# Wide bf16 products of the identity in the waits of TensorE through the heads loop of a three-layer block kernel

## Chip, cores and metric

One core of one Trainium2 chip runs the whole program. The metric is the device time of one execution in microseconds (us), the median of several; smaller is better. The profile shows one execution on the same core. Engine names: PE is TensorE's matmul, PEld its weight load, DVE VectorE, ACT ScalarE, POOL GpSimd, SP SyncE.

## What is computed

The reference runs one sequence of 256 tokens of width 1024 through three layers: a gated delta rule mixer with 16 value heads and 8 key heads of width 128, a forgetting attention with 16 heads of width 64, and a block with window attention, pooling and a layer of 16,384 small experts. The change touches the first alone, and of it the part per head:

```
g = cumsum(g);  decay = exp(where(lower, g_t - g_s, -inf))
L = where(strict, (k*beta) @ k.T * decay, 0)
T = inverse(I + L)                  # unit lower triangular
u, w = T @ (v*beta), T @ (k*beta*exp(g))
v_new = u - w @ state;  o = (q*exp(g)) @ state + (q @ k.T * decay) @ v_new
state = state * exp(g_last) + k_dec.T @ v_new
```

The kernel takes chunks of 128 tokens, two per sequence, where the reference has 64; the result is the same.

## The kernel before, in words

The program is written by hand for each engine, with semaphores between them: within an engine the order of the code is the order of the work. Every projection is made of fp32r products of high and low parts. The input projection of the delta rule runs until about 195 us, then comes the **heads loop**, then the output projection.

The heads loop has 8 rounds (`rounds(inner)`, L2544). A round takes one key head and its two value heads g = 0, 1. In `inner(i, f, n)` (L2496) three rounds are in flight: `i` is the one whose triangular matrices are inverted, `f` the one before it, which is finished, and `n` the one after, which is set up. So round 0 has no `f`, and round 7 has no `n`; the finish of round 7 stands after the loop, between the output products.

The inverse of the four 128x128 matrices (two heads, two chunks) is built up in six levels j = 0 to 5, from blocks of 2 to one of 128. A level has two halves. `level_p(r, j)` (L2413) waits for the semaphores `h_xx` (the matrix so far, `XC` and its transpose `XC_T`) and writes into the PSUM bank PA; DVE's `mask_level` (L1648) masks it into SBUF and fires `h_pm`; `level_d(r, j)` (L2438) multiplies again into the bank PB; DVE's `close_level` (L1660) subtracts and fires `h_xx`, twice a level (three times at level 4, once at level 5, 12 in a round). For j < 4 each half is 16 products of 32x32 blocks (PE L2424 and L2451, two records each), at j = 4 it is 8 and 12 small ones (L2429; L2456, L2458), at j = 5 four of 64x64 (L2434, L2462). DVE's parts of them: L1653 is the mask of levels 0 to 3, L1656 of level 4, L1658 of level 5; L1664 closes levels 0 to 3, L1669 and L1671 level 4, L1674 level 5.

Between these halves PE does the rest of the three rounds in a fixed order:

- `finish(f, 0)` to `finish(f, 5)` (L2466): 128x128 fp32 products, steps 0, 1, 2, 3 at L2474, L2478, L2481, L2484, step 4 with three products for each head (L2489 to L2491), step 5 at L2494. The copies between them are ACT's (L965 after step 0, L968 after step 1).
- `setup_keys(n)` (L2375), `setup_rows(n)` (L2364; two bf16 products of 512 columns at L2372, a selector column against BG3), `setup_values(n)` (L2388; four transposes at L2393), `setup_low(n)` (L2399; 16 small products at L2402, after DVE's `lowers`, L1638).
- `modulator(i)` (L2406; two fp32 products of one column at L2410, of rows that POOL has summed) and, while `i.at + 2 < 8`, `norm_sums` (L2352; one fp32 product of 512 columns at L2356, which the trace shows as two).

BG3 is a bf16 tile of 128 rows by 512 columns that holds the gate rows in high, middle and low parts (48 of the 128 rows; the rest is zero); it is written before the loop and only read in it. `ident16` is the 128x128 identity in bf16. `mm` is `pe.matmul(out, stationary, moving)`. A PSUM bank is 512 fp32 columns; PA is ps[2], PB is ps[3].

At round 7 ACT has work of another kind: `late_silu` (L896), for which it loads another table of functions (L898) and then the old one again (L752). DVE and ACT also split the operand of the output projection into parts in that round (L1405, L766).

`keep_clock` (L2286) makes small fp32 products of the identity at three places outside the loop; the loop has none.

Of the kernel before, what the change touches and what calls it, by code (L numbers as in the profile page):

```python
# [51 lines left out]
def program(nc, x, c, norm_w, ada_w, ada_b, a_w_in, a_conv_w, a_A_log, a_dt_bias, a_norm_w, a_w_out,  # L52
# [4 lines left out]
    with ctx:  # L57
# [3 lines left out]
        def sem(name):  # L61
            return ctx.enter_context(nc.semaphore(name))
# [11 lines left out]
        def at(off, n, tensor=AR):  # L74
            return tensor[:, off:off + n]
# [14 lines left out]
        def small(n, p=P):  # L90
            pos[0] += n
            assert pos[0] <= 2624, pos[0]
            return SMALL[0:p, pos[0] - n:pos[0]]
# [3 lines left out]
        ident16 = small(64).bitcast(B16)  # L97
# [78 lines left out]
        h_p, h_pm, h_d, h_xx = sem("h_p"), sem("h_pm"), sem("h_d"), sem("h_xx")  # L176
# [156 lines left out]
        BG3 = at(T0 + 10496, 256).bitcast(B16)  # L333
# [32 lines left out]
        PA, PB, PBC = ps[2], ps[3], ps[3][:, 256:320]  # L366
# [1861 lines left out]
        def _(pe):  # L2228
            mm = pe.matmul
# [134 lines left out]
            def setup_rows(r):  # L2364
                pe.wait_ge(g_kks, r.count(1, 1))
                pe.wait_ge(g_kqs, r.count(1, 1))
                pe.wait_ge(g_k0s, r.count(1, 1))
                if r.at:
                    pe.wait_ge(h_bv, r.count(4))
                for g in range(2):  # L2370
                    h = r.heads[g]
                    mm(ROWS[g][:, :], SELB[:, h:h + 1].broadcast_to([P, P]), BG3, start=True, stop=True).then_inc(h_row, 1)  # L2372

            def setup_keys(r):
                pe.wait_ge(g_norm, r.count(2, 2))  # L2375
                pe.wait_ge(ada_free, r.count(1, 9))
                if r.at == 0:
                    pe.wait_ge(g_ln, 2)
                for cc in range(2):
                    kc = r.k[:, cc * 128:cc * 128 + 128]  # L2380
                    ins = mm(KKP[:, cc * 128:cc * 128 + 128], kc, kc, start=True, stop=True)
                ins.then_inc(g_kk, 1)
                for cc in range(2):
                    chunk = slice(cc * 128, cc * 128 + 128)
                    mm(KQP[:, cc * 128:cc * 128 + 128], r.k[:, chunk], r.q[:, chunk], start=True, stop=True)
                pe.transpose(K0P, r.k[:, 0:128], ident).then_inc(g_k0, 1)

            def setup_values(r):  # L2388
                for g in range(2):
                    pe.wait_ge(h_eg, r.nth(g))  # L2390
                    pe.wait_ge(h_xm, r.nth(g))
                    for cc in range(2):
                        ins = pe.transpose(ROWS[g][:, 256 + cc * 128:384 + cc * 128], r.v[g][:, cc * 128:cc * 128 + 128], ident)  # L2393
                    ins.then_inc(h_vT, 1)

            def diagonal_blocks():
                return [(m, q, m // 2, 128 * (m % 2) + q) for m in range(4) for q in (0, 32, 64, 96)]

            def setup_low(r):  # L2399
                pe.wait_ge(h_lt, r.nth(1))  # L2400
                for m, q, g, at_ in diagonal_blocks():
                    ins = mm(LOWC[q:q + 32, 32 * m:32 * m + 32], LT[r.side][g][q:q + 32, at_:at_ + 32], ident[q:q + 32, q:q + 32],  # L2402
                             start=True, stop=True)
                ins.then_inc(h_xT, 1)

            def modulator(r):  # L2406
                pe.wait_ge(mod_sum, r.count(15, 24 + 15))
                pe.wait_ge(ada_free, r.count(1, 10))
                for cc in range(2):
                    ins = mm(MODP[:, cc:cc + 1], RAW[MOD_SLOT[r.side]][:, 0, cc * 128:cc * 128 + 128], ones[:, 0:1], start=True, stop=True)  # L2410
                ins.then_inc(raw_free, 1)

            def level_p(r, j):  # L2413
                lt = LT[r.side]
                if j == 0:
                    pe.wait_ge(h_xt, r.count(3, 2))
                elif j < 5:
                    pe.wait_ge(h_xx, r.count(12, 2 * j - 1))
                else:
                    pe.wait_ge(h_xx, r.count(12, 9))  # L2420
                    pe.wait_ge(h_spread, r.count(6, 2))
                if j < 4:
                    for m, q, g, at_ in diagonal_blocks():
                        ins = mm(PA[q:q + 32, 32 * m:32 * m + 32], lt[g][q:q + 32, at_:at_ + 32], XC[q:q + 32, m, :],  # L2424
                                 start=True, stop=True)
                elif j == 4:
                    for m, q, g, at_ in diagonal_blocks():
                        if q % 64 == 0:
                            ins = mm(PA[q + 32:q + 64, 32 * m:32 * m + 32], lt[g][q:q + 32, at_ + 32:at_ + 64], XC[q:q + 32, m, :],  # L2429
                                     start=True, stop=True)  # L2430
                else:
                    for m in range(4):
                        at_ = 128 * (m % 2)
                        ins = mm(PA[64:128, 64 * m:64 * m + 64], lt[m // 2][0:64, at_ + 64:at_ + 128], XPAIR[0:64, m, :],  # L2434
                                 start=True, stop=True)
                ins.then_inc(h_p, 1)

            def level_d(r, j):  # L2438
                pe.wait_ge(h_pm, r.count(6, j + 1))
                if j == 0:  # L2440
                    pe.wait_ge(h_xt, r.count(3, 3))
                    if r.at:
                        pe.wait_ge(h_xx, r.count(12))
                elif j < 5:
                    pe.wait_ge(h_xx, r.count(12, 2 * j))
                else:
                    pe.wait_ge(h_xx, r.count(12, 11))
                    pe.wait_ge(h_spread, r.count(6, 4))
                if j < 4:
                    for m, q, g, at_ in diagonal_blocks():  # L2450
                        ins = mm(PBC[q:q + 32, 16 * m:16 * m + 16], XC_T[q:q + 32, m, :], PC[q:q + 32, 16 * m:16 * m + 16],  # L2451
                                 start=True, stop=True)
                elif j == 4:
                    for m in range(4):
                        pm = PC[:, 32 * m:32 * m + 32]
                        mm(PB[32:64, 32 * m:32 * m + 32], XC_T[32:64, m, :], pm[32:64, :], start=True, stop=True)  # L2456
                        for q in (0, 64):
                            ins = mm(PB[q:q + 32, 128 + 32 * m:160 + 32 * m], pm[q + 32:q + 64, :], XC_T[q + 32:q + 64, m, :],  # L2458
                                     start=True, stop=True)
                else:  # L2460
                    for m in range(4):
                        ins = mm(PB[0:64, 64 * m:64 * m + 64], XPAIR[64:128, m, :], INVT[r.side][64:128, m, 64:128],  # L2462
                                 start=True, stop=True)
                ins.then_inc(h_d, 1)
# [30 lines left out]

            def inner(i, f, n):  # L2496
                level_p(i, 0)
                level_d(i, 0)
                if f:
                    finish(f, 0)  # L2500
                level_p(i, 1)
                if f:
                    finish(f, 1)
                if n:
                    setup_keys(n)
                level_d(i, 1)
                if f:
                    finish(f, 2)
                level_p(i, 2)
                if n:  # L2510
                    setup_rows(n)
                level_d(i, 2)
                if f:
                    finish(f, 3)
                level_p(i, 3)
                if f:
                    finish(f, 4)
                level_d(i, 3)
                if n:
                    setup_values(n)  # L2520
                level_p(i, 4)
                level_d(i, 4)
                if f:
                    finish(f, 5)
                if n:
                    setup_low(n)
                level_p(i, 5)
                modulator(i)
                if i.at + 2 < GQ:
                    norm_sums(Round(i.at + 2))  # L2530
                level_d(i, 5)
# [203 lines left out]
            for half in range(2):  # L2735
                for b in range(2):
                    for kk in range(4 * half, 4 * half + 4):
                        for n, (w, xx) in enumerate(((WHI, XHI), (WHI, XLO), (WLO, XHI))):
                            ins = mm(bank(T_AUP, 3)[:, b * S:b * S + S], w[:, slot, kk, b * P:b * P + P], xx[:, (kk + 4) % KC, :],
                                     start=(kk == 0 and b == 0 and n == 0), stop=(kk == KC - 1 and n == 2), skip_group_check=True)  # L2740
# [4 lines left out]
            for half in range(2):  # L2745
                pe.wait_ge(x_split, 17 + half)
                for t in range(TT):
                    for kk in range(4 * half, 4 * half + 4):
                        for n, (xx, w) in enumerate(((XHI, WHI), (XLO, WHI), (XHI, WLO))):
                            ins = mm(bank(T_WO, 0)[:, t * TW:t * TW + TW], xx[:, (kk + 4) % KC, t * P:t * P + P], w[:, slot, kk, :],  # L2750
                                     start=(kk == 0 and t == 0 and n == 0), stop=(kk == KC - 1 and n == 2), skip_group_check=True)
# [158 lines left out]
```

## Time and profile before

| | us |
|---|---|
| median of 3 runs | 1623.2 |
| lowest and highest | 1621.7, 1625.29 |
| time of the profiled execution | 1621.4 |
| its span, first to last instruction | 1619.6 |
| mean granted TensorE clock in it | 0.987 of full |
| PE busy | 1554.8 |
| DVE busy | 1109.9 |
| ACT busy | 932.7 |

The share of busy PE is high over the span, but a busy PE isn't one at its peak: the matmuls are pipelined and their ends are modelled, so the time from one start to the next tells more than a duration. In the chain of waits a piece runs until the next one of the chain begins, so its pieces add up. The granted clock is given as a share of full speed: 1.00 is 2.4 GHz, 0.50 is 1.2 GHz.

### The profile page before, as it was taken

To read this page: it belongs to the slowest core of one execution; us is meant where nothing else is said; L and a number is where in the kernel's file an instruction comes from. 1 tells how busy PE (TensorE), PEld (TensorE's weight loads), DVE (VectorE), ACT (ScalarE), POOL (GpSimd) and SP (SyncE) were. 2 spreads that over 40 slices of the span, in tenths; PEclk is the share of its full clock that TensorE was granted. 3 is DMA by queue.
4 is the path that set the end of the run, shared out by engine and by line. 5 is a ranking of instruction groups with operands and counts; after the bars stand their busy time and mean duration, and the time that the engine had idled before them with its cause. 6 is when DMAs were issued, how large, how long until landed. Compare 5 with 4: busy or idle time off the path is not lost.

```text
span 1619.6 us, 37025 instructions
## 1 busy us (share of the span) xinstructions
PE 1554.8 (96%) x13269; PEld 1429.3 (88%) x13269; DVE 1109.9 (69%) x2304; ACT 932.7 (58%) x1763; POOL 493.4 (30%) x405
## 2 busy tenths in 40 slices
PE   7899999899999999999999999999999999999998
PEld 6899877798998899888999999999999888888886
DVE  3787768656556653776478888798888555555554
ACT  1766567744555555545354444799898544555554
POOL 4000278661000040000067777766565100000000
PEclk9999979899999999999999999999999999999999
DMA  9668412454443344247455555544444666666663
GB/s 295 219 184 278 150 55 82 133 163 130 151 131 118 111 156 131 79 157 156 104 150 167 168 168 172 162 143 135 140 131 143 182 194 194 193 192 190 194 193 127
DMA packets 211832, 255.89 MB, mean 158 GB/s; under 512 B 15912, under 2 KB 193804, under 8 KB 211724
## 3 DMA queue, kind: packets, MB, share of 16 engines
q1 hardware_dynamic: 211723, 254.39, 53.2%
q8 instruction: 76, 1.25, 0.3%
q14 instruction: 33, 0.26, 0.1%
HBM read 253.29 MB, written 1.05 MB: 157 GB/s over the span
## 4 chain that ended last, share of the span: by engine, by line
PE 72%; DVE 11%; issue 5%; DMA 4%; ACT 4%; SPq 2%; DVEq 0%; ACTq 0%
PE ps L2253 22%; PE ps L2861 22%; PE ps L2843 10%; PE ps L2831 3%; DMA raw<-in_u_experts 3%; PE ps L2273 2%; PE ps L2551 2%; DVE raw L2014 2%; SPq L580 2%; PE ps L2628 1%; DVE w_lo L1396 1%; PE ps L2451 1%; DMA arena<-in_ada_w 1%; DVE arena L2067 1%; PE ps L2648 1%
## 5 line engine op out<-in xcount | busy, mean ns | idle before, releaser
L742 POOL TENSOR_TENSOR w_lo<-raw,w_hi 128x1024 fp32r<-128x1024 f32 x128 | 307.6, 2406 | 337.7 <-ACT w_hi L1265 337.6
L2253 PE MATMUL ps<-x_hi,w_hi 128*128 128x256 f32 x1088 | 315.3, 290 | 8.3 <-DVE w_lo L1396 3.0
L2253 PE MATMUL ps<-x_hi,w_lo 128*128 128x256 f32 x1088 | 308.2, 283 | 0.0
L2253 PE MATMUL ps<-x_lo,w_hi 128*128 128x256 f32 x1088 | 308.2, 283 | 0.0
L2212 DVE TENSOR_TENSOR w_lo<-raw,w_hi 128x1024 fp32r<-128x1024 f32 x124 | 152.0, 1226 | 143.2 <-ACT w_hi L1374 143.2
L1374 ACT ACTIVATE w_hi<-raw 128x1024 fp32r<-128x1024 f32 x124 | 131.6, 1061 | 168.0 <-PE ps L2861 168.0
L2253 PEld LDWEIGHTS ps<-x_hi,w_hi 128*128 128x128 f32 x1088 | 209.1, 192 | 15.3 <-issue 6.0
L2253 PEld LDWEIGHTS ps<-x_lo,w_hi 128*128 128x128 f32 x1088 | 209.2, 192 | 1.3 <-issue 1.2
L2253 PEld LDWEIGHTS ps<-x_hi,w_lo 128*128 128x128 f32 x1088 | 209.0, 192 | 0.0
L1265 ACT ACTIVATE w_hi<-raw 128x1024 fp32r<-128x1024 f32 x128 | 134.9, 1054 | 113.4 <-DVE raw L2014 113.2
L2806 PE MATMUL ps<-x_hi,w_hi 128*128 128x256 f32 x576 | 166.3, 289 | 10.6 <-ACT arena L1287 9.7
L2014 DVE STREAM_TRANSPOSE raw<-raw 128x1024 f32<-128x1024 f32 x128 | 158.3, 1237 | 17.1 <-DMA raw<-in_u_experts 15.8
L2806 PE MATMUL ps<-x_lo,w_hi 128*128 128x256 f32 x576 | 162.8, 283 | 0.0
L2806 PE MATMUL ps<-x_hi,w_lo 128*128 128x256 f32 x576 | 162.7, 282 | 0.0
L2861 PE MATMUL ps<-w_hi,x_hi 128*128 128x512 f32 x512 | 157.6, 389 | 1.1 <-DVE x_lo L2202 1.1
L2861 PE MATMUL ps<-w_lo,x_hi 128*128 128x512 f32 x512 | 157.7, 389 | 0.0
L2861 PE MATMUL ps<-w_hi,x_lo 128*128 128x512 f32 x512 | 157.6, 389 | 0.0
L1396 DVE TENSOR_TENSOR w_lo<-arena,w_hi 128x2048 fp32r<-128x2048 f32 (+1 forms) x43 | 97.1, 2258 | 70.0 <-ACT w_hi L759 70.0
L1396 DVE TENSOR_TENSOR w_lo<-raw,w_hi 128x2048 fp32r<-128x2048 f32 (+1 forms) x43 | 97.2, 2261 | 69.3 <-ACT w_hi L759 69.3
L2843 PE MATMUL ps<-x_lo,w_hi 128*128 128x256 f32 x448 | 131.9, 294 | 0.0
L2843 PE MATMUL ps<-x_hi,w_hi 128*128 128x256 f32 x448 | 126.7, 283 | 0.0
L2843 PE MATMUL ps<-x_hi,w_lo 128*128 128x256 f32 x448 | 126.5, 282 | 0.0
(446 smaller groups left out, 3563.7 us busy)
## 6 DMA issues: line engine op xcount, KB each, us to landing
raw<-in_u_experts SPq DMA_DIRECT2D x512, 128.0 KB, 2.7
raw<-in_v_experts SPq DMA_DIRECT2D x128, 512.0 KB, 4.3
arena<-in_ada_w SPq DMA_DIRECT2D x18, 1024.0 KB, 7.8
raw<-in_a_w_in SPq DMA_DIRECT2D x12, 1024.0 KB, 5.7
arena<-in_a_w_in SPq DMA_DIRECT2D x12, 1024.0 KB, 5.7
raw<-in_b_w_in SPq DMA_DIRECT2D x8, 1024.0 KB, 5.7
arena<-in_b_w_in SPq DMA_DIRECT2D x8, 1024.0 KB, 5.6
raw<-in_w_in SPq DMA_DIRECT2D x8, 1024.0 KB, 5.6
```

The lines of the kernel that those rows point to most:

```text
L580: sp.dma_start(URAW[u][32 * q:32 * q + 32, :].rearrange("p (a c) -> p a c", a=4), src).then_inc(u_in[u], 16)
L742: pool.tensor_tensor(UTL[e], UT[e % 2], UTH[e].bitcast(F32), ALU.subtract).then_inc(utl_ready, 1)
L1265: act.activation(UTH[e % 4], UT[e % 2], ACT.Copy).then_inc(uth_ready, 1)
L1374: act.activation(VH[u], VRAW[u], ACT.Copy).then_inc(high_ready, 1)
L1396: v.tensor_tensor(WLO[:, slot, 0:k, :], RAW[raw_slot(base, u)][:, 0:k, :], WHI[:, slot, 0:k, :].bitcast(F32), ALU.subtract).then_inc(lo_re ...
L2014: v.transpose(UT[s_].rearrange("p (k a j) -> p a k j", k=KC, a=4), URAW[s_].rearrange("p (a k i) -> p a k i", a=4, k=KC)).then_inc(ut_read ...
L2212: v.tensor_tensor(VL[u], VRAW[u], VH[u].bitcast(F32), ALU.subtract).then_inc(low_ready, 1)
L2253: ins = mm(o[:, b * S:b * S + S], w[:, slot, kk, b * P:b * P + P], xx[:, (kk + turn) % KC, :], start=(kk == 0 and n == 0), stop=(kk == k - ...
L2806: ins = mm(ps[e % 2][:, 0:S], w[e % 4][:, kk * P:kk * P + P], xx[:, kk, :], start=(kk == 0 and n == 0), stop=(kk == KC - 1 and n == 2))
L2831: ins = mm(GB.rearrange("p (e t) -> p t e", t=4)[:, q, :], OHJ[:, c % 2, q, :], OHI[:, c % 2, q, :], start=True, stop=True, skip_group_che ...
L2843: ins = mm(ps[e % 2][:, 0:S], w[e % 4][:, kk * P:kk * P + P], xx[:, kk, :], start=m == 0, stop=m == 23)
L2861: ins = mm(ps[4 + 2 * t + h][:, :], g[:, u, t * P:t * P + P], w[u][:, 512 * h:512 * h + 512], start=False, stop=False, skip_group_check=True)
```

## The change

A helper `keep_wide(bank_, n)` issues n products of `ident16` with BG3 over the whole of a PSUM bank, whose result nobody reads. `level_p` calls it on PA before its waits, `level_d` on PB before its wait for `h_pm`; the number is an argument, `spare`, given in `inner` by the place in the round and by whether there is an `f` or an `n`. In `level_d` at level 0 the wait for the last `h_xx` of the round before moves ahead of it, since the products overwrite PB.

```diff
--- before.py
+++ after.py
@@ -2410,8 +2410,13 @@
                     ins = mm(MODP[:, cc:cc + 1], RAW[MOD_SLOT[r.side]][:, 0, cc * 128:cc * 128 + 128], ones[:, 0:1], start=True, stop=True)
                 ins.then_inc(raw_free, 1)
 
-            def level_p(r, j):
+            def keep_wide(bank_, n):
+                for _ in range(n):
+                    mm(bank_[:, :], ident16, BG3, start=True, stop=True)
+
+            def level_p(r, j, spare=0):
                 lt = LT[r.side]
+                keep_wide(PA, spare)
                 if j == 0:
                     pe.wait_ge(h_xt, r.count(3, 2))
                 elif j < 5:
@@ -2435,12 +2440,13 @@
                                  start=True, stop=True)
                 ins.then_inc(h_p, 1)
 
-            def level_d(r, j):
+            def level_d(r, j, spare=0):
+                if j == 0 and r.at:
+                    pe.wait_ge(h_xx, r.count(12))
+                keep_wide(PB, spare)
                 pe.wait_ge(h_pm, r.count(6, j + 1))
                 if j == 0:
                     pe.wait_ge(h_xt, r.count(3, 3))
-                    if r.at:
-                        pe.wait_ge(h_xx, r.count(12))
                 elif j < 5:
                     pe.wait_ge(h_xx, r.count(12, 2 * j))
                 else:
@@ -2495,36 +2501,36 @@
 
             def inner(i, f, n):
                 level_p(i, 0)
-                level_d(i, 0)
+                level_d(i, 0, 2)
                 if f:
                     finish(f, 0)
-                level_p(i, 1)
+                level_p(i, 1, 0 if f else 2)
                 if f:
                     finish(f, 1)
                 if n:
                     setup_keys(n)
-                level_d(i, 1)
+                level_d(i, 1, 0 if n else 1)
                 if f:
                     finish(f, 2)
-                level_p(i, 2)
+                level_p(i, 2, 0 if f else 2)
                 if n:
                     setup_rows(n)
-                level_d(i, 2)
+                level_d(i, 2, 0 if n else 2)
                 if f:
                     finish(f, 3)
-                level_p(i, 3)
+                level_p(i, 3, 0 if f else 2)
                 if f:
                     finish(f, 4)
-                level_d(i, 3)
+                level_d(i, 3, 0 if f else 2)
                 if n:
                     setup_values(n)
-                level_p(i, 4)
-                level_d(i, 4)
+                level_p(i, 4, 0 if n else 2)
+                level_d(i, 4, 1)
                 if f:
                     finish(f, 5)
                 if n:
                     setup_low(n)
-                level_p(i, 5)
+                level_p(i, 5, 0 if f else 2)
                 modulator(i)
                 if i.at + 2 < GQ:
                     norm_sums(Round(i.at + 2))
```

## Rows read from the trace of the kernel before

**Rows 1.** The page's first line, the profiled execution:

```profile
span 1619.6 us, 37025 instructions
```

**Rows 2.** Chosen stretches: length, busy us (instructions) by engine, granted clock, DMA share, GB/s:

```profile
203.10:220.20 17.10, 15.23 (x276) 11.97 (x277) 8.26 (x25) 7.73 (x25) 14.35 (x22) 0.50 0.21 64
...
290.20:293.60 3.40, 3.40 (x86) 2.42 (x86) 3.17 (x10) 2.88 (x8) 3.40 (x7) 1.00 0.11 24
305.50:308.90 3.40, 2.68 (x85) 2.28 (x84) 3.17 (x10) 3.27 (x10) 3.40 (x7) 1.00 0.80 257
308.90:322.60 13.70, 11.95 (x252) 10.14 (x252) 5.78 (x17) 7.74 (x15) 6.46 (x9) 0.50 0.77 245
```

**Rows 3.** Timeline of PE, round 0: start us, us, line, operation, shapes, idle before:

```profile
197.20 0.44 PE L2451 MATMUL ps<-arena 32*32 32x16 f32 x32 [0.43 <-DVE arena L1653]
197.99 0.45 PE L2424 MATMUL ps<-arena 32*32 32x32 f32 x32 [0.35 <-DVE arena L1664]
...
201.02 0.61 PE L2372 MATMUL ps<-arena,small 128*128 128x512 bf16 x2 [0.20 <-DVE arena L1627]
201.56 0.44 PE L2451 MATMUL ps<-arena 32*32 32x16 f32 x32
```

**Rows 4.** Chain that ended last, rounds 0 to 2, 5, 6: start us, us, what:

```profile
203.47 0.63 PE ps L2451 x32
204.10 1.04 PE ps L2393 x4
205.14 0.59 PE ps L2429 x16
...
207.51 0.65 PE ps L2402 x32
...
214.02 0.63 PE ps L2451 x32
...
222.04 0.64 PE ps L2484 x4
...
223.48 0.22 PE ps L2490 x2
...
224.60 0.37 PE ps L2451 x32
224.97 0.59 PE ps L2393 x4
225.56 0.39 PE ps L2429 x16
...
231.34 0.33 DVE arena L1674
...
231.86 0.44 PE ps L2451 x32
...
279.05 0.44 PE ps L2451 x32
...
294.34 0.44 PE ps L2451 x32
```

**Rows 5.** Timeline of PE, end of round 1 (columns as in rows 3):

```profile
227.76 0.45 PE L2402 MATMUL ps<-small,arena 32*32 32x32 f32 x32
...
230.25 0.68 PE L2462 MATMUL ps<-arena 64*64 64x64 f32 x8
```

**Rows 6.** Chain that ended last, round 7 (columns as in rows 4):

```profile
310.77 1.28 ACT L752
...
312.39 1.22 PE ps L2478 x4
...
319.91 0.43 PE ps L2490 x2
...
322.94 0.46 PE ps L2429 x16
```

**Rows 7.** Waits of PE, 196 to 330: line, releaser, total us, times, longest:

```profile
PE ps L2456 <- DVE arena L1656: 3.2, 8, 0.4
```

## The prediction

> **What bounds the kernel now.** I read three things in this order: the page's head, then the granted clock of chosen stretches, then the chain of work that ended last beside the timeline of PE. The profiled execution spans 1619.6 us [rows 1]; the program's own time for it is 1621.4, so 1.8 us lie around the span, and it stands 1.8 us under the median of the runs, 1623.2. I take all savings against that execution and subtract their sum from the median. About 0.2%, 3.2 us, is what a measurement of this kernel can tell from no change.
>
> The clock: over 203.1 to 220.2 and over 308.9 to 322.6 TensorE was granted 0.50 of full speed, its 1.2 GHz level; elsewhere in the loop, as at 290.2 and 305.5, 1.00, which is 2.4 GHz [rows 2]. The first lies over the end of round 0 and most of round 1, the second over round 7. What the engine did before the second fall can be set beside a twin: 305.5 to 308.9 belongs to the same part of round 6 as 290.2 to 293.6 of round 5, 15.3 us earlier. There the clock held. Both have a PE busy most of the time by instructions [rows 2], but only the earlier one holds the two 512-column products of `norm_sums`, which rounds 6 and 7 leave out; the later has only 32- and 64-row blocks and the one-column products of `modulator`. So what I read is that small blocks don't keep the clock and wide products do. Round 0 has no `finish` work of an earlier round, so it too is nearly all small blocks.
>
> The chain: in the loop it alternates between PE products and short DVE masks in round 0, and runs almost wholly over PE from d0 to p4 in rounds 1 to 6 (I call level_p and level_d at step j of a round p_j and d_j). Start to start from the d0 of round 1 to that of round 2 is 231.86 - 214.02 = 17.84 us, the first part at the low clock; from round 5 to round 6 it is 294.34 - 279.05 = 15.29 [rows 4].
>
> **The change.** Nothing is removed. It adds 39 products of the bf16 identity with BG3, 512 columns each: 13 in round 0, 3 in each of rounds 1 to 6 (a pair in d0, one in d4), 8 in round 7 (d0 2, d1 1, d2 2, p4 2, d4 1). It moves one wait: in d0 of rounds 1 to 7 the wait for `h_xx` now stands before the pair, since the pair overwrites PB. No DMA, no SP or POOL instruction moves.
>
> *Price of a pair.* The nearest row is `setup_rows`, two bf16 128x128 by 512-column products: 201.02 to the next start at 201.56, 0.54 us at the full clock [rows 3]. A single one is then 0.27. They have different stationary operands; the new ones share theirs, so it could be a little less. By the Trainium skill (TensorE: Matmul & The Clock Gate, Back-to-back issue gap) a sustained stream of 512-column products has about 131 ns each, a pair 0.26; the rows have twice that, and I keep the rows.
>
> *Round 0 before the fall.* The pairs at d0, p1, p2, p3 and d3 stand in waits for DVE. d0 starts at 197.20 and p1 at 197.99, 0.79 apart [rows 3], of which a 32-block level issues for 0.37 (at 224.60) [rows 4]; 0.42 is left for 0.54. So +0.12 each at p1 and p2, and about as little at d0 (0.03); p3's is swallowed, since DVE computes `decays` there, and so is d3's. Sum +0.27.
>
> *Round 0 from 203.1, if the clock holds.* Cold against warm durations of the same work: d3 0.63 to 0.37, `setup_values` 1.04 to 0.59, p4 0.59 to 0.39: -0.91 [rows 4]. Then DVE, unchanged. From `setup_low` at 207.51 to the d0 of round 1 at 214.02 it took 6.51 [rows 4]. Warm: `setup_low` to d5 is 230.25 - 227.76 = 2.49 [rows 5]; add the pair at p5, 0.54; d5 itself, 0.68; DVE's L1674, at least 0.33 [rows 4] and with its handovers 0.5; the pair of d0, 0.54: 4.75. That is -1.76. With the +0.27 the stretch gives **-2.4**.
>
> *Round 1, d0 to d0.* 17.84 becomes 15.29: **-2.55**.
>
> *The pair in d0, rounds 2 to 6.* This is the cost. L1674 on DVE ends at 231.34 + 0.33 = 231.67 and fires `h_xx`; the mask follows, and d0 starts at 231.86 [rows 4]. So the moved wait leaves a gap of 0.19 us and not more, and 0.54 must fit in it: +0.35 per round. Behind it on PE stands d0, and everybody waits for d0, since from here the chain is PE's. Five rounds, **+1.75**. Bounds: nothing (it fits) to 0.54 each, 2.7 in all; I take 0.35 because both ends of the gap are rows. The d0 of round 7 is hidden: the next finish step there starts at 312.39 because ACT loads tables and does the late silu until 312.05 [rows 6]. The single in d4 stands in the eight waits for DVE's L1656, 3.2 us in total, 0.4 each after the modelled end of the products [rows 7]; it costs 0.
>
> *Round 7, if the clock holds.* Up to 312.39 ACT sets the pace and nothing is gained. From there to p4 at 322.94 the PE issues finish steps 1, 2 and 3, each four pieces, at 1.22 us cold against 0.64 warm: -1.74; the levels d1, p2, d2, p3 and d3 at about 0.63 against 0.37: -1.3; and the six products of finish step 4 at 0.43 against 0.22: -1.26 [rows 4, 6]. Together -4.3. Against that: the single at d1 lies on the path, 0.27; the pairs at d2 and p4 exceed their waits by 0.12 each, by the gap of round 0. **-3.8**, with half of the 4.3 as the lower bound, should DVE and ACT set the pace for part of the way.
>
> What is late next: in round 7 the copies of ACT and the masks of DVE, which I count at the gaps above; after the loop PE works on the output products from operands that the same rounds make. No row shows another engine or a load taking over there, so I let the shift through to the end undiminished; what it would lose if one did is left to the range.
>
> Sum: -2.4 - 2.55 + 1.75 - 3.8 = -7.0, so 1623.2 - 7.0 = **1616.2**.
>
> **Rivals.**
> *A. The last fall stays.* For it: in round 6 the change puts one product at d4, about 304, and then nothing until the pair of d0, which waits for L1674 and so comes at about 294.34 + 15.29 - 0.2 = 309.4 [rows 4]. The stretch of [rows 2] from 305.5 to 308.9 stays as it was. Against: a wide product now stands close on either side of it. Then round 7 gives no gain and its wide products cost about 1.8 times (cold against warm `setup_values`, 1.04 to 0.59 [rows 4]), 0.97 a pair: the single at d1 0.48, the pairs at d2 and p4 0.97 - 0.42 each, in all +1.6. Sum -2.4 - 2.55 + 1.75 + 1.6 = -1.6: 1621.6, not to be told from no change.
> *B. The first fall comes later and is short.* After d3 the PE has transposes, p4, one wide product and d4 only, until the pair at p5. If the clock falls there, some 2 us of the 4.95 of rounds 0 and 1 are lost: -5.0, 1618.2.
> *C. Slower: neither holds.* The place is d0 and p5. If the products are too sparse, each round still pays 0.35, and those in cold stretches pay 0.97 a pair: +0.27 + 0.97 + 0.78 in rounds 0 and 1, +1.75, +1.6 in round 7, in all +5.4: 1628.6. It decides once both stretches are cold for as long as now. Against it: round 0 gets thirteen wide products, and rounds 1 to 6 held the clock with fewer.
> *D. The pairs fit their gaps.* The d0 pair is one reload of the same operand; if two take no more than the 0.19 us gap plus what the queue hides, the +1.75, the +0.27, the +0.51 of round 7 and some 0.7 of the pairs at p5 and d0 of round 1 go: -10.2, 1613.0. The Trainium skill's rule above points there; the 0.54 of the rows speaks against it.
>
> **How the numbers follow.** Forecast 0.48, A 0.20, B 0.16, C 0.08, D 0.08. Forecast, B and D are faster by over 0.2%: 0.72; A is the same: 0.20; C is slower: 0.08. The range takes in the forecast with its bounds (the d0 pair at nothing gives 1614.5, at 0.54 each 1617.2, half the gain of round 7 1618.3), A and B, and most of D with the spread of the runs: 1612.5 to 1621.8. C is left out.
>
> **What would show it.** The granted clock at 1.00 over 196 to 328. d0 to d0 of round 1 at about 15.6, and of rounds 3 to 5 at 15.6 rather than 15.29, with the pair standing between L1674 and d0. `setup_low` to the next d0 at 4.8 in round 0. In round 7 the finish steps at 0.64. It is wrong if a stretch at 0.50 remains in round 7 (A), or near 206 to 212 (B), or if the d0 spacing stays at 15.3 (D) or grows beyond 15.9.

## The result, and the profile after

The changed kernel is slower, not faster: 1625.36 us median of 20 runs (1621.88 to 1629.12) against 1622.42 of 20 runs of the kernel before (1620.03 to 1626.52), ratio 1.0018 with a 95% interval of 1.001 to 1.0025. That is +2.9 us where -7.0 was forecast, and outside the range. The profiled execution took 1629.12, the longest of the 20; it is read for where things stand, not for its length. In what follows a wide product is one of 512 columns.

Its first lines:

```profile
span 1627.4 us, 37075 instructions
...
PE 1560.8 (96%) x13280; PEld 1433.4 (88%) x13308; DVE 1112.9 (68%) x2304; ACT 933.1 (57%) x1763; POOL 492.7 (30%) x405
```

Chosen stretches of the changed kernel, columns as in [rows 2]:

```profile
203.20:208.30 5.10, 3.52 (x142) 2.22 (x131) 4.21 (x12) 3.97 (x15) 4.94 (x8) 1.00 0.02 6
208.40:222.00 13.60, 12.94 (x185) 9.41 (x191) 4.77 (x15) 3.37 (x10) 10.45 (x17) 0.50 0.25 79
...
310.70:314.10 3.40, 1.86 (x45) 1.42 (x46) 2.83 (x8) 3.34 (x7) 3.40 (x6) 1.00 1.06 359
314.20:327.80 13.60, 12.31 (x254) 10.15 (x257) 5.63 (x16) 6.75 (x15) 5.19 (x8) 0.50 0.68 216
```

Both falls of the clock are still there. The first now comes at 208.4, 10.8 us after the first p0 (it was 6.8 us after it), and lasts until 222.0; the second comes at 314.2 and lasts until 327.8, as long as that of [rows 2]. One profile is one draw: in the five kernels below whose round 0 has no added product (moved_wait, d0_single, d0_pairs_only, fill_last, late_d5) the first fall comes 2.6 to 6.8 us after the first p0, and in the four that have the round 0 of the change up to p5 and keep the pair there (the change, dense_data, no_d0_pairs, other_bank) 10.8 to 13.3 us after it. So the added products put the fall off and don't prevent it.

The stretch ahead of each fall is the thing to see. PE's instructions kept it busy for 3.52 of 5.10 us and for 1.86 of 3.40. The timeline of PE around the first shows what they were:

```profile
206.00 0.44 PE L2434 MATMUL ps<-arena 32*32 32x32 f32 x16
...
208.39 0.65 PE L2402 MATMUL ps<-small,arena 32*32 32x32 f32 x32 [1.10 <-DVE arena L1638]
209.37 0.63 PE L2415 MATMUL ps<-arena,small 128*128 128x512 bf16 x1 [0.33 <-DVE arena L1671]
209.93 1.11 PE L2439 MATMUL ps<-arena 64*64 64x64 f32 x8
...
211.84 2.06 PE L2356 MATMUL ps<-arena,small 128*128 128x512 f32 x2
...
215.86 0.63 PE L2415 MATMUL ps<-arena,small 128*128 128x512 bf16 x1 [0.34 <-issue]
216.42 0.62 PE L2457 MATMUL ps<-arena 32*32 32x16 f32 x32
```

Between p4 at 206.00 and the pair of p5, whose second product stands at 209.37, there is no wide product but the single one of d4, whose matmul isn't in the records (its weight load is, at 206.37). From the fall on everything costs about double: the pair ahead of p5, `modulator`, `norm_sums` at 2.06 us (1.10 in a round at the full clock), and the pair ahead of d0 of round 1.

Ahead of the second fall it is the same. These are the weight loads of the added products between the d4 of round 6 and the fall at 314.2:

```profile
307.71 0.10 PEld L2415 LDWEIGHTS ps<-arena,small 128*128 128x128 bf16 x1
313.58 0.11 PEld L2415 LDWEIGHTS ps<-arena,small 128*128 128x128 bf16 x2 [0.72 <-DVE arena L1674]
```

For 5.9 us there is none, and the pair that comes 0.6 us ahead of the fall doesn't stop it.

The two answers to [rows 4] and [rows 5]: `setup_low` of round 0 to the d0 of round 1 takes 216.42 - 208.39 = 8.03 us (6.51 before, 4.75 forecast); round 1, d0 to d0, 18.09 (17.84 before, 15.29 forecast). In rounds 4 to 6, all at the full clock, d0 to d0 takes 15.86 where it took 15.29. How that comes about, in the changed kernel and, below it, in the kernel before (timeline of all engines, lines around d0 of round 5; L1674 is the last `close_level` of the round before):

```profile
281.41 0.41 DVE L1674 TENSOR_SCALAR arena<-ps 64x256 f32<-64x256 f32 x1
...
281.87 0.11 PEld L2415 LDWEIGHTS ps<-arena,small 128*128 128x128 bf16 x2 [0.53 <-DVE arena L1674]
...
282.41 0.44 PE L2457 MATMUL ps<-arena 32*32 32x16 f32 x32
```

```profile
278.46 0.41 DVE L1674 TENSOR_SCALAR arena<-ps 64x256 f32<-64x256 f32 x1
...
279.05 0.44 PE L2451 MATMUL ps<-arena 32*32 32x16 f32 x32 [0.54 <-DVE arena L1653]
```

From the start of L1674 to d0 it is 1.00 us instead of 0.59: +0.41. The other 0.16 stands a little further on: DVE's `normalised_k`, L1615, which `setup_keys` waits for, takes twice as long in six of its eight executions, those that stand in the loop. By line, before and after (count, duration in ns min/median/max, first and last start):

```profile
L1615 DVE TENSOR_TENSOR arena<-arena x8: 418/467/471, 184.8 to 295.5; 128x256 f32<-128x256 f32 x8
```

```profile
L1615 DVE TENSOR_TENSOR arena<-arena x8: 417/938/946, 186.1 to 299.3; 128x256 f32<-128x256 f32 x8
```

The cause can be read from the traces. In the loop a `tensor_tensor` of POOL is always running when L1615 starts. The one of round 5, before and after (timeline of POOL and of DVE):

```profile
279.65 0.79 POOL L696 TENSOR_TENSOR raw<-raw 128x256 f32<-128x256 f32 x1
280.26 0.47 DVE L1615 TENSOR_TENSOR arena<-arena 128x256 f32<-128x256 f32 x1
```

```profile
283.36 0.72 POOL L696 TENSOR_TENSOR raw<-raw 128x256 f32<-128x256 f32 x1
283.42 0.94 DVE L1615 TENSOR_TENSOR arena<-arena 128x256 f32<-128x256 f32 x1
```

Before, L1615 ends at 280.73, 0.29 us after POOL's instruction (280.44); after, at 284.36, 0.28 after it (284.08). In 80 of the 84 executions of L1615 in the loops of all 14 traces it ends 0.28 to 0.29 us after the POOL instruction that was running when it started; in the other four that one had at most 0.04 us to go. So L1615 lasts for what is left of POOL's instruction and 0.28 us more: 0.19 is left of it before, 0.66 in the change, where the later L1615 meets the start of an instruction instead of its end.

The table has the same spans, read from PE's timeline, and the stretches at 1.2 GHz for each kernel's one profile. R0 is the first p0 to the d0 of round 1, R1 that d0 to the next, R2-6 the d0 of round 2 to that of round 7, Rn the median spacing of rounds 4 to 6, R7 the d0 of round 7 to the finish step after the loop. The last column is the median over all executions of the time at the low clock, 2 x (1 - mean granted clock) x span, in the whole program.

| kernel | ratio to before | R0 | R1 | R2-6 | Rn | R7 | low clock in the loop | low, us |
|---|---|---|---|---|---|---|---|---|
| before | 1 | 17.70 | 17.84 | 77.76 | 15.29 | 18.33 | 203.1 to 220.2, 308.9 to 322.6 | 42 to 45 |
| the change | 1.0018 | 18.82 | 18.09 | 79.61 | 15.86 | 18.99 | 208.4 to 222.0, 314.2 to 327.8 | 36 |
| moved_wait | 1.0015 | 18.73 | 17.33 | 77.75 | 15.33 | 18.27 | 199.0 to 219.5, 311.6 to 321.8 | 44 |
| d0_single | 1.0000 | 18.91 | 17.21 | 77.99 | 15.47 | 17.59 | 198.9 to 219.4, 311.5 to 321.7 | 44 |
| d0_pairs_only | 1.0026 | 19.24 | 17.36 | 80.19 | 15.85 | 17.64 | 200.5 to 221.0, 313.2 to 326.9 | 49 |
| no_d0_pairs | 0.9989 | 16.74 | 15.28 | 77.52 | 15.31 | 18.61 | 211.4 to 214.8, 306.9 to 320.6 | 32 |
| dense_data | 1.0020 | 17.33 | 18.18 | 79.59 | 15.86 | 18.88 | 211.2 to 221.4, 313.6 to 327.3 | 36 |
| other_bank | 1.0001 | 16.85 | 18.09 | 77.35 | 15.29 | 19.07 | 211.1 to 221.3, 310.0 to 323.7 | 34 |
| low_wait_filled | 0.9988 | 15.02 | 15.82 | 79.80 | 15.86 | 18.13 | 313.2 to 320.0 | 23 |
| late_d5 | 0.9998 | 17.72 | 17.85 | 77.70 | 15.29 | 18.36 | 202.9 to 220.0, 312.2 to 322.4 | 39 |
| fill_last | 0.9989 | 18.69 | 17.33 | 77.62 | 15.28 | 18.09 | 199.1 to 219.6, 318.6 to 322.0 | 31 |
| fill_first | 0.9969 | 14.78 | 15.67 | 77.27 | 15.29 | 17.83 | 306.7 to 316.9 | 26 |
| fill_gaps | 0.9965 | 14.80 | 15.67 | 77.26 | 15.29 | 20.98 | 316.0 to 326.2 | 16 |
| fill_all_rounds | 0.9960 | 14.90 | 15.57 | 77.55 | 15.29 | 21.12 | 318.7 to 328.9 | 8 |

Each ratio is against executions of the kernel before on the same chip; their medians were 1622.67 (31 runs, first group of experiments), 1622.12 (35) and 1620.62 (29). A difference in us below is taken from the ratio, so that the three chips can be set beside each other.

R2-6 doesn't follow from Rn alone. In each trace one round, the second or the third, is longer than its neighbours, in most of them by a stall in which PE waits for nothing that the trace shows. It is longest in the kernel before, in round 3:

```profile
251.72 0.29 PE L2451 MATMUL ps<-arena 32*32 32x16 f32 x10 [1.13 <-issue]
```

That round takes 16.60 us there, 1.3 more than the next. In the change it is round 2, with 0.3 more. In the four kernels with the pair into PB the longer round has 0.3 to 0.5 us more, in all others 0.6 to 1.3, so that over rounds 2 to 6 the change is 1.85 us behind the kernel before and not five times 0.57. Why the stall is shorter with the pairs no run shows.

### The profile page after: what moved, and what is told of

Read it like the earlier page. It is cut to its first block, busy times and chain, and to the rows that moved or that the text cites. A ratio compares the mean times of both kernels' runs of the same rounds, so it can differ in the third digit from the quotient of the medians.

```text
span 1627.4 us, 37075 instructions
## 1 busy us (share of the span) xinstructions
PE 1560.8 (96%) x13280; PEld 1433.4 (88%) x13308; DVE 1112.9 (68%) x2304; ACT 933.1 (57%) x1763; POOL 492.7 (30%) x405
## 4 chain that ended last, share of the span: by engine, by line
PE 73%; DVE 12%; issue 5%; DMA 4%; ACT 4%; SPq 2%; DVEq 0%; another core or an unknown queue 0%; ACTq 0%
PE ps L2867 21%; PE ps L2253 21%; PE ps L2849 10%; PE ps L2837 3%; DMA raw<-in_u_experts 3%; PE ps L2273 2%; PE ps L2557 2%; DVE raw L2014 2%; SPq L580 1%; PE ps L2634 1%; DVE w_lo L1396 1%; PE ps L2457 1%; DVE arena L2067 1%; PE ps L2300 1%; PE ps L2654 1%
## 5 line engine op out<-in xcount | busy, mean ns | idle before, releaser
L2253 PE MATMUL ps<-x_lo,w_hi 128*128 128x256 f32 x1088 | 308.9, 284 | 0.0
L2253 PE MATMUL ps<-x_hi,w_lo 128*128 128x256 f32 x1088 | 308.9, 284 | 0.0
L1374 ACT ACTIVATE w_hi<-raw 128x1024 fp32r<-128x1024 f32 x124 | 131.6, 1061 | 167.9 <-PE ps L2867 167.9
```

The costliest lines, as they stand in the source:

```text
L1374: act.activation(VH[u], VRAW[u], ACT.Copy).then_inc(high_ready, 1)
L2253: ins = mm(o[:, b * S:b * S + S], w[:, slot, kk, b * P:b * P + P], xx[:, (kk + turn) % KC, :], start=(kk == 0 and n == 0), stop=(kk == k - ...
```

## The experiments

Three questions. Do these products keep the clock at all? What does the pair in d0 cost, and why? Which stretches let the clock fall?

**dense_data.** The same products with a moving operand that is dense.

```diff
-                    mm(bank_[:, :], ident16, BG3, start=True, stop=True)
+                    mm(bank_[:, :], ident16, X[:, 0, 0:512].bitcast(B16).rearrange('p (n two) -> p n two', two=2)[:, :, 1], start=True, stop=True)
```

> The whole change, but the moving operand is 512 columns of bf16 halves of the residual rows, dense in all 128 rows, instead of BG3, of which 48 rows are not zero. Theory S: nothing changes, 1.0018 of before, and the clock falls in the same two places. Theory Z (products of an operand of mostly zeros do not keep the clock): the low clock in rounds 0, 1 and 7 goes or shrinks to under 5 us each, and the time is 5 us or more under that of the change.

1625.47 us, 1.0020 (1.0006 to 1.0034); the clock fell in both places, and the spacing was 15.86. BG3's zeros are not the matter.

**d0_pairs_only** and **no_d0_pairs** share out the 39 products. In the first, `inner` is that of before but for:

```diff
-                level_d(i, 0)
+                level_d(i, 0, 2 if f else 0)
```

and in the second, against the change:

```diff
-                if j == 0 and r.at:
-                    pe.wait_ge(h_xx, r.count(12))
                 keep_wide(PB, spare)
                 pe.wait_ge(h_pm, r.count(6, j + 1))
                 if j == 0:
                     pe.wait_ge(h_xt, r.count(3, 3))
+                    if r.at:
+                        pe.wait_ge(h_xx, r.count(12))
...
-                level_d(i, 0, 2)
+                level_d(i, 0, 0 if f else 2)
```

> Only the moved wait and the pair in d0 of rounds 1 to 7 are kept; the other 25 wide products are gone. Theory S (sparse: the products leave stretches without any, the clock falls as before, and each pair in d0 stands on the path): the clock falls at 203 to 208 and at about 309 to 314 in the profile, and the time is that of before plus 6 to 7 times 0.35, 1.0014 of before, 2.0 to 2.8 us slower. Theory H (the pairs hide in waits; the loss of the whole change comes from its first and last rounds): within 0.5 us of before.

> The whole change without the pairs in d0 of rounds 1 to 7, the wait back in its old place; 25 wide products stay (13, 6 singles in d4, 6 in round 7). Theory S: the time of before within 1 us, or a little above it (0 to +1.5 us), since the clock still falls in round 0 after d3 and at the end of round 6. Theory H: as slow as the whole change, +2.9 us.

The pairs alone: 1626.90, 1.0026 (1.0015 to 1.0037), +4.2 us, more than forecast; spacing 15.85. Without them: 1619.88, 0.9989 (0.9976 to 1.0001), so the other 25 products gain a little under 2 us, which their interval can just not tell from nothing, and the pairs cost it all and more. Neither expectation was met: the gain was in neither theory. In its profile the first low stretch is down to 211.4 to 214.8; the second is unchanged.

**moved_wait** and **d0_single** take the d0 apart: the wait alone (no product at all), and with one product (the edit below, against the kernel before, beside the moved wait).

```diff
-                level_d(i, 0)
+                level_d(i, 0, 1 if f else 0)
```

> Only the moved wait of the change, no wide product at all. Theory S (the pair costs, not the wait): within 0.5 us of before, d0 to d0 in rounds 3 to 6 stays at 15.3 us. Rival W (the wait for h_xx ahead of the others costs a handover of its own): spacing above 15.4 and +1 us.

> The moved wait and one product instead of two in d0 of rounds 1 to 7, nothing else. By the sum of a row each (0.27 to 0.31 for one, against a gap of 0.19): spacing 15.4 to 15.5, 0.5 to 1.5 us above before. If the doubled duration of DVE's L1615 (0.94 against 0.47 us) comes with any late d0, it is there too and the spacing is 15.55 or more; if it hangs on where DVE's instruction falls beside POOL's, it may be gone.

One product: 1620.66, 1.0000 (0.9991 to 1.0009), spacing 15.47, and L1615 in it:

```profile
L1615 DVE TENSOR_TENSOR arena<-arena x8: 418/466/749, 184.9 to 296.0; 128x256 f32<-128x256 f32 x8
```

It is back at 0.47 us in five of the six executions in the loop; the first takes 0.75, at 216.44, and again ends 0.28 us after the POOL instruction that it met (216.19 to 216.91). So one wide product ahead of d0 costs 0.18 us a round and doesn't shift L1615 onto the start of a POOL instruction; two cost 0.41 and do. The second product alone is then 0.23. What the traces show is this order in time; no run took POOL's work away.

The wait alone: 1624.73, 1.0015 (1.0003 to 1.0027), some 2.4 us slower, which was not expected. Its spacing of 15.33 to 15.38 accounts for 0.3 us of it; and the kernel with one product, which has the same wait, is at 1.0000. The profiled execution can't show the rest, as it took 1621.0, the second shortest of the ten. I can't name it. It also means that part of what d0_pairs_only costs may not be the pairs'.

**other_bank.** The pair of d0 goes to a bank that nobody reads at that point, so it needs no wait; the wait for `h_xx` is back in its old place.

```diff
-                level_d(i, 0, 2)
+                if f:
+                    keep_wide(ps[4], 2)
+                level_d(i, 0, 0 if f else 2)
```

> The whole change with one difference: in rounds 1 to 7 the pair of d0 is written into ps[4], which nobody reads at that point, so that it stands ahead of the wait for h_xx, which is back in its old place. Theory Q (the pair is dear because it must follow h_xx, 0.19 us before d0 can start): d0 to d0 returns from 15.86 to 15.3 us, and the time is that of the change less 7 times 0.57, 0.9985 to 0.9995 of before. Rival E (a wide pair costs its 0.54 wherever it stands): the spacing stays at 15.7 or more and the time within 1 us of the change.

1620.49 against 1620.62, 1.0001 (0.9989 to 1.0013), 2.8 us under the ratio of the change. Timelines of PE and of DVE around the d0 of round 5:

```profile
279.01 0.38 PE L2415 MATMUL ps<-arena,small 128*128 128x512 bf16 x1 [0.16 <-issue]
279.41 0.44 PE L2457 MATMUL ps<-arena 32*32 32x16 f32 x32
```

```profile
278.82 0.41 DVE L1674 TENSOR_SCALAR arena<-ps 64x256 f32<-64x256 f32 x1
```

The second product of the pair starts at 279.01 while L1674 still runs; d0 starts 0.59 us after the start of L1674, as in the kernel before, and the spacing is 15.29. The same 512 columns twice cost nothing there. So it was not the 0.54 us of the pair, it was the place: the choice of PB made it wait for the last reader of PB. The spacing came out as expected; the time fell by 2.8 us where four (7 times 0.57) were.

**low_wait_filled.** In round 0 the pair ahead of p5 becomes three ahead of `setup_low`.

```diff
-                level_p(i, 5, 0 if f else 2)
+                level_p(i, 5)
```

```diff
+                if not f:
+                    keep_wide(PA, 3)
                 if n:
                     setup_low(n)
```

> The whole change, but in round 0 the pair ahead of p5 becomes three products ahead of setup_low, in the 0.8 to 1.1 us for which PE waits there for DVE. Theory G (the gap between d3 and p5 of round 0 is what lets the clock fall at 206 to 211): the fall in rounds 0 and 1 goes in most executions, and the time is 2 to 3.5 us under that of the change. If it is the number of products and not the gap: within 1 us of the change.

1618.66, 0.9988 (0.9980 to 0.9997): 4.9 us under the ratio of the change, more than expected, with one product more than it. The median time at the low clock falls to 23 us. Timeline of PE, and the stretch that was cold before:

```profile
206.23 0.44 PE L2434 MATMUL ps<-arena 32*32 32x32 f32 x16
...
207.44 0.82 PE L2415 MATMUL ps<-arena,small 128*128 128x512 bf16 x3
208.62 0.45 PE L2402 MATMUL ps<-small,arena 32*32 32x32 f32 x32 [0.36 <-DVE arena L1638]
...
212.84 0.44 PE L2457 MATMUL ps<-arena 32*32 32x16 f32 x32
```

```profile
208.40:222.00 13.60, 12.85 (x353) 10.26 (x355) 8.59 (x31) 7.95 (x27) 11.57 (x19) 1.00 0.25 80
```

The three stand where PE was idle, `setup_low` starts 2.39 us after p4 as it did (2.39 in the change), and the clock stays at 1.00. From `setup_low` to d0 it is 4.22 us instead of 8.03.

**fill_gaps, fill_first, fill_last, late_d5.** From the kernel before, without the moved wait: products in PE's idle times, and in the stretches that had none. `spare(bank, a, b)` issues a products in round 0 and b in round 7; `late` is rounds 6 and 7. fill_first has only what belongs to round 0, fill_last only what belongs to rounds 6 and 7, with three more products after the loop, and late_d5 only the three ahead of d5 in round 6. Excerpt:

```diff
+                spare(PA, 3, 0)
                 level_p(i, 0)
+                spare(PB if head else ps[7], 1, 2)
                 level_d(i, 0)
...
+                spare(ps[7], 0, 4)
                 if f:
                     finish(f, 1)
...
+                spare(PA, 3, 0)
                 if n:
                     setup_low(n)
...
+                if late:
+                    pe.wait_ge(h_bv, 4 * GQ)
+                    keep_wide(ps[7], 3)
                 level_d(i, 5)
```

> The kernel before, with wide products only where the trace has PE idle, and in the stretches that had none: round 0 has 3 before p0, 1 each before d0, p1, p2, p3, 2 before d3, 1 before d4, 3 before setup_low; rounds 6 and 7 have 3 before d5, where rounds 0 to 5 have norm_sums; round 7 has 2 before d0 and 4 before finish step 1 into a bank nobody reads, 1 each before d2, p4, d4; 3 stand before the finish step after the loop. Nothing in rounds 1 to 5, no wait moved. Theory S: the clock stays at 1.00 from 196 to 330 and the time falls by 6 to 9 us, 0.995 of before. Theory Z: the clock falls in both places as before and the time is 0 to 2 us above before.

> The 13 products of round 0 of the kernel that fills the gaps, nothing else. Theory S: the clock stays at 1.00 from 196 to 222 in most executions, first p0 to the d0 of round 2 in 30.5 us where the kernel before takes 35.5; median 3 to 5 us under before. Rival L (it was the last rounds that gave the 6 us): within 1.5 us of before.

> Only the products of rounds 6 and 7 and after the loop of the kernel that fills the gaps (17). Theory S: the fall near 309 goes in most executions or comes later and is shorter; median 1.5 to 4 us under before. Rival F (it was the first rounds alone): within 1 us of before.

> Three wide products ahead of the d5 of round 6 and nothing else: in place of the norm_sums which that round leaves out, in a wait for DVE of 0.7 us. If the missing wide products of round 6 are what lets the clock fall at 309, as the comparison with round 5 suggests, this takes back half or more of what the 17 products of the last rounds do (1 to 3 us), the fall moving into round 7 where ACT holds PE up; if round 7 is too sparse by itself, the clock falls 3 to 4 us later and the time is within 1 us of before.

fill_gaps: 1616.20, 0.9965 (0.9954 to 0.9976), -5.7 us. fill_first: 1616.43, 0.9969 (0.9957 to 0.9981), -5.0. fill_last: 1619.74, 0.9989 (0.9977 to 1.0001), -1.8. late_d5: 1621.26, 0.9998 (0.9985 to 1.0011). The first rounds bring most. fill_gaps missed its expectation for the clock, which still falls once in its profile, at 316.0; the time is at the low end of it (6.5 us between the medians, 5.7 by the ratio, where 6 to 9 were). fill_first and late_d5 came as expected, fill_last at the low end, with an interval that reaches no change. Chosen stretches of late_d5, and two lines of its PE timeline:

```profile
305.50:308.90 3.40, 3.09 (x83) 2.19 (x69) 3.20 (x10) 3.29 (x8) 3.40 (x6) 1.00 0.93 293
308.90:312.20 3.30, 1.58 (x69) 1.28 (x69) 2.08 (x7) 3.26 (x5) 3.22 (x6) 0.99 1.10 349
312.20:322.50 10.30, 9.51 (x184) 8.10 (x184) 3.52 (x11) 4.36 (x11) 3.04 (x5) 0.50 0.64 202
```

```profile
306.72 0.81 PE L2415 MATMUL ps<-arena,small 128*128 128x512 bf16 x3
...
312.13 1.23 PE L2482 MATMUL ps<-arena 128*128 128x128 f32 x4 [1.19 <-ACT arena L965]
```

With three wide products, the stretch 305.5 to 308.9, at whose end the clock fell in [rows 2], passes in this execution; the clock falls 3.3 us later, at the end of the next one, where finish step 1 waits 1.19 us for ACT. Filling one gap moves the fall to the next.

**fill_all_rounds.** fill_gaps with a pair into ps[4] ahead of d0 of rounds 1 to 6 as well.

> The kernel that fills the gaps, with a pair in ps[4] ahead of d0 of rounds 1 to 6 in addition. Theory Q: spacing stays at 15.3 and the time within 1 us of the kernel that fills the gaps (1616.2), since rounds 1 to 6 hold the clock without it. Theory E: 3 us slower than that kernel.

1613.38 of 6 runs against 1620.62, 0.9960 (0.9947 to 0.9972); against fill_gaps (0.9965) no difference that the intervals can tell. Both beat the kernel before and the change. What is left in the profile of fill_gaps stands in round 7, in the middle of one level's products (timeline of PE):

```profile
313.64 0.36 PE L2455 MATMUL ps<-arena 32*32 32x16 f32 x21
315.56 0.30 PE L2455 MATMUL ps<-arena 32*32 32x16 f32 x11 [1.55 <-issue]
```

PE stands for 1.55 us between the 21st and the 22nd product of d3 with no releaser, and the clock falls at 316.0, 0.4 us behind it. fill_all_rounds has one of 1.8 us in round 7, fill_last one of 2.07, low_wait_filled one of 1.1, moved_wait, which has no added product at all, one of 0.9, and the kernel before one of 0.3. The three longest are in the three kernels with the same added products in round 7. Their cause is not settled. Busy DMA engines are not what it takes: in fill_last the DMA share during the stall is 1.07 and in fill_gaps 0.03, and during the 1.13 us of the kernel before in round 3 it is 0.00.

## Why the prediction was wrong, step by step

**The clock holds: failed.** The forecast rested on it, at 0.48, and both falls stayed. Nearly the whole miss is here. By the profiles, with the forecast beside them: R0 +1.1 (-2.4), R1 +0.3 (-2.55), R2-6 +1.85 (+1.75), R7 +0.7 (-3.8). (The pair of round 2 stands in R1, those of rounds 3 to 7 in R2-6.) Together the loop takes 135.5 us against 131.6, +3.9, where -7.0 was summed.

The step behind it is the reading that a wide product close on either side keeps the clock. I had the places right: rival A, no product between d4 of round 6 and the pair of d0, and rival B, only one after d3 until p5. What came is both at once, which is rival C, both stretches cold and nearly as long as before (27 us in the loop of the profile against 31), and C had 0.08 and was left out of the range. Its price of +5.4 was too high: rounds 0 and 1 lost 1.4 where C has 2.0, rounds 2 to 6 1.85 where it has 1.75, and round 7 0.7 where it has 1.6.

B's price was too low: I took 2 of the 4.95 us as lost. Measured, the first p0 to the d0 of round 2 takes 36.91 us against 35.54, so everything was lost and 1.4 more. It is made up of +0.16 up to d3, -0.56 from there to `setup_low`, since the fall comes later, +0.96 at the pair ahead of p5 and +0.55 at that ahead of d0, both at 1.2 GHz, and +0.25 in round 1. `norm_sums` is no part of it: it ran at the low clock before too.

The twin stretches of [rows 2] also differ in more than I said. The one of round 5 has PE busy for 3.40 of 3.40 us, the one of round 6 for 2.68, so they can't tell small products from idle time; and the fillers of the experiments put in both width and work. One stretch of the kernel before shows that busy time alone doesn't tell where the clock falls (columns as in [rows 2]):

```profile
248.30:251.70 3.40, 2.29 (x67) 1.98 (x65) 2.25 (x5) 1.93 (x8) 3.32 (x5) 1.00 0.26 89
```

It has less busy time than 305.5 to 308.9, an idle time of 1.13 us and no wide product, but 128x128 fp32 products (`finish` step 1 and `setup_keys`), and the clock held. That speaks for the size of the products, from one place in one execution; no run fills a wait with small products, so whether the width or the filled time did it stays open.

**The pair in d0: mis-sized.** The term was 0.35 a round; in the rounds 4 to 6 it is 0.57. 0.05 of the difference is the wake-up of PE after the wait, which I had left out of the 0.19 gap (L1674 ends at 281.82, the first weight load starts at 281.87), and 0.16 comes from L1615 on DVE, which runs into the start of a POOL instruction. That the pair stands on the path and that rounds 1 to 6 don't hide it was right. My upper bound of 0.54 was still too low for such a round. That R2-6 grew by 1.85, near the 1.75 of the sum, is luck: five times 0.57 is 2.85, and the shorter stall gave 1.0 back, of which I knew nothing. The pair of round 7 delays its d0 like the others (15.85). That the wait for ACT behind it takes the delay back, as I said, is likely: R7 is 17.64 in d0_pairs_only and 17.59 in d0_single against 18.33, one profile each.

**What was right.** The pairs in round 0's waits: +0.27 forecast, +0.16 measured from p0 to d3 (7.31 against 7.15). The single product in d4 costs nothing: with it (no_d0_pairs) the spacing is 15.31 against 15.28 to 15.29. The price of a pair, 0.54 us: 281.87 to 282.41. Wide products in PE's waits can keep the clock: the kernels that fill the gaps show it for round 0 (1.00 from 196 to 222, R0 from 17.70 to 14.80). What fill_first gains, 5.0 us (5.1 over R0 and R1 in its profile), is near the 4.95 forecast for the same rounds. The Trainium skill (TensorE: Matmul & The Clock Gate, Back-to-back issue gap) gives some 131 ns for each 512-column product of a long stream. The traces here disagree: 0.54 us for a pair with its weight load, 0.27 each, and within the group of three in low_wait_filled one starts 0.22 us after the other (207.44, 207.66).

**The account.** The change lowers the median time at the low clock from 42 to 45 us to 36, and still costs 2.9. What 1 us less at the low clock gives is an estimate from the runs that only add fillers: fill_first 16 us less for 5.0, 0.31 for each, fill_gaps 29 for 5.7, 0.20, fill_last 11 for 1.8, 0.16. So 6 to 9 us less give back 1.0 to 2.8; the pairs take 3.4 to 4.0 (six or seven times 0.57), less the shorter stall; the two pairs of rounds 0 and 1 that run at the low clock take some 1 to 1.5. That comes to +0.6 to +4.5, and 2.9 lies within it. It fits, but so wide a sum is no test.

## What to carry to other kernels

A filler must be judged by its gaps, not by its number: look for the longest stretch without a wide product, waits for other engines included, and put the filler there; one left open gave the clock away here for 10 to 20 us in most profiles, in which the pair ahead of p5 cost 0.96 us instead of 0.54. A filler needs an output that nobody is reading: if it shares a buffer with the work it stands beside, it inherits that buffer's wait and moves from the idle time onto the path. And when two rivals rest on the same cause in two places, they are not independent: the case that has both (C here, at 0.08) deserves a chance near that of each alone, and a place in the range. Last, look at what the neighbours do at the instant where an instruction will start: a shift of 0.4 us put DVE's L1615 behind a whole POOL instruction.

## What the runs showed of the hardware

- DVE's `tensor_tensor` over 128x256 fp32 (L1615) takes 0.42 us with no POOL instruction beside it (28 executions ahead of the loop) and 0.38 to 0.95 in the same position of a round, by how long the `tensor_tensor` of POOL that it meets still runs: it ends 0.28 to 0.29 us after that one, in 80 of 84 cases.
- The records of PE lose many of the added products: 39 weight loads but 18 matmuls are on the line, and a pair that stands behind small blocks shows only its second one. The time between starts has both in it. Line L2415 of the changed kernel (count, ns min/median/max, first and last start):

```profile
L2415 PEld LDWEIGHTS ps<-arena,small x39: 95/98/151, 198.0 to 328.5; 128*128 128x128 bf16 x39
L2415 PE MATMUL ps<-arena,small x18: 379/379/634, 198.2 to 328.5; 128*128 128x512 bf16 x18
```

- PE can stand for up to 2.07 us inside a group of products without a releaser. Every trace has such a stall or a stretched group in round 2 or 3, and six of them one of 0.5 us or more in round 7; the DMA share during those read ranges from 0.00 to 1.09. The longest were in the three kernels with the most added products in round 7; whether that is the reason no run shows.
